# Delta rule of an RWKV-7 layer: the last level's growth interleaved with z's products, spreading behind the level's first products, and the masks for the sample chunk shared among engines

## What is computed

```python
def step(S, inp):
    r_t, w_t, k_t, v_t, kk_t, b_t = inp
    sa = jnp.einsum('bhvk,bhk->bhv', S, kk_t)
    S = S * w_t[:, :, None, :] - sa[..., None] * b_t[:, :, None, :] + v_t[..., None] * k_t[:, :, None, :]
    return S, jnp.einsum('bhvk,bhk->bhv', S, r_t)
```

## Time and profile before

| | us |
|---|---|
| timed executions | 1428.38, 1430.29, 1417.46 |
| their median | 1428.38 |
| profiled execution, its own time | 1415.87 |
| its span, first to last instruction | 1414.1 |

### The profile page before, as it was taken

One profiled execution on the slowest core, in us unless ns is written; L12 is line 12 of the kernel. 1 busy time (PEld: TensorE's weight loads), 2 busy tenths in 40 slices (PEclk: granted clock), 3 DMA queues, 4 the chain that ended last, 5 costly groups with the idle time before them and its releaser, 6 DMA issues. The chain is left out here.

```text
span 1414.1 us, 33194 instructions
## 1 busy us (share of the span) xinstructions
PE 1341.6 (95%) x13740; PEld 1178.7 (83%) x13740; DVE 768.3 (54%) x1571; ACT 634.4 (45%) x1486; POOL 240.8 (17%) x335
## 2 busy tenths in 40 slices
PE   7999999999999998999999799999999998998997
PEld 6989999888899977888887388899999997665885
DVE  6837434677771047898888444721121113776445
ACT  6725445778762124445544432521111134876224
POOL 0000000000000045777776200000001000113000
PEclk9999999999999989999999999999999998999999
DMA  6722313466679255666773381053334265330212
GB/s 215 229 66 67 105 62 115 116 176 220 194 209 268 67 110 105 134 138 145 157 156 81 116 297 54 1 203 92 92 92 111 62 167 180 101 103 24 91 41 86
DMA packets 265272, 178.44 MB, mean 126 GB/s; under 512 B 169600, under 2 KB 239168, under 8 KB 264208
## 3 DMA queue, kind: packets, MB, share of 16 engines
q1 hardware_dynamic: 233159, 161.37, 40.1%
q10 hardware_dynamic: 31968, 15.04, 3.7%
HBM read 116.21 MB, written 60.46 MB: 125 GB/s over the span
## 5 line engine op out<-in xcount | busy, mean ns | idle before, releaser
L369 PE MATMUL mix_acc<-mix_high,mix_w_high 128*128 128x364 f32 (+1 forms) x768 | 178.2, 340 | 12.3 <-ACT mix_high L435 9.9
L369 PE MATMUL mix_acc<-mix_low,mix_w_high 128*128 128x364 f32 (+1 forms) x768 | 172.0, 332 | 1.2 <-DVE mix_low L589 1.2
L369 PE MATMUL mix_acc<-mix_high,mix_w_low 128*128 128x364 f32 (+1 forms) x768 | 170.8, 331 | 0.0
L369 PEld LDWEIGHTS mix_acc<-mix_high,mix_w_high 128*128 128x128 f32 x768 | 130.1, 189 | 31.5 <-issue 28.3
L369 PEld LDWEIGHTS mix_acc<-mix_low,mix_w_high 128*128 128x128 f32 x768 | 132.9, 189 | 2.3 <-DVE mix_low L589 2.1
L369 PEld LDWEIGHTS mix_acc<-mix_high,mix_w_low 128*128 128x128 f32 x768 | 133.6, 189 | 0.2 <-DVE mix_w_low L603 0.2
L603 DVE TENSOR_TENSOR mix_w_low<-mix_wt,mix_w_high 128x1024 fp32r<-128x1024 f32 x32 | 39.2, 1224 | 126.0 <-ACT mix_w_high L441 125.7
L1605 PE MATMUL out_acc<-qkvg_room_r_high,qkvg_room_w_high 128*128 128x364 f32 (+1 forms) x320 | 105.8, 331 | 1.2 <-DVE qkvg_room_w_low L1957 1.2
L1605 PE MATMUL out_acc<-qkvg_room_r_low,qkvg_room_w_high 128*128 128x364 f32 (+1 forms) x320 | 105.1, 329 | 0.0
L1605 PE MATMUL out_acc<-qkvg_room_r_high,qkvg_room_w_low 128*128 128x364 f32 (+1 forms) x320 | 105.1, 328 | 0.0
L455 ACT ACTIVATE mix_out<-mix_acc 128x364 f32<-128x364 f32 (+1 forms) x96 | 38.3, 471 | 144.8 <-PE mix_acc L369 144.7
(11 more groups left out here) (282 smaller groups left out, 3110.6 us busy)
## 6 DMA issues: line engine op xcount, KB each, us to landing
mix_wt<-in_w_in SPq DMA_DIRECT2D x32, 512.0 KB, 4.4
qkvg_room_wt<-in_w_att SPq DMA_DIRECT2D x20, 512.0 KB, 3.6
delta_bk<-scr_bk SPq DMA_DIRECT2D x68, 128.0 KB, 3.5
delta_kr<-scr_kr SPq DMA_DIRECT2D x17, 512.0 KB, 6.7
scr_kr<-mix_outs SPq DMA_DIRECT2D x16, 512.0 KB, 3.6
scr_bk<-mix_outs SPq DMA_DIRECT2D x16, 512.0 KB, 4.4
early_xpad<-in_xpad SPq DMA_DIRECT2D x8, 548.5 KB, 8.5
scr_xg<-early_xs SPq DMA_DIRECT2D x8, 544.0 KB, 3.2
```

What stands on the lines that cost most here:

```text
L369: mm = pe.matmul(acc[:, s, k, 0:width], w[:, s, d, :], r[:, d, n0:n0 + width], start=d == 0 and q == 0, stop=d == DT - 1 and q == 2)
```

## The change

1. `make_lm` of level 0 writes each head's product to the other half of the partitions, and `keep_lm` copies it back in two halves, so `lm_kept` counts eight a chunk (`lm_copies`). `begin_z` and `end_z` write to the other half too, and `keep_z` copies z back in two halves.
2. `end_z` goes pair by pair between the pairs of the last level's `grow`.
3. `spread_blocks` of the front chunk stands behind the level-2 `make_lm`.
4. On ScalarE the root stands ahead of the first row copy; on VectorE the masks of the front chunk's first Gram products stand ahead of the last solving steps.
5. At the end GpSimd masks v for four sequences and ScalarE for four; ScalarE masks u for four and VectorE for four; VectorE makes the plain copy of u in halves, alternating with ScalarE's. z's products of the sample chunk stand ahead of the own products 0 and 1, and five warm products are gone.
6. VectorE makes one low part of weights instead of two after each of the pairs 4 to 7; the other four are made in the next stage, behind the first tokens' low part.

```diff
@@ -907,6 +907,10 @@
     return ap.rearrange("p (m o b) -> p m o b", o=2, b=8 << lev)[:, :, odd, :]
...
+def lm_copies(c, lev, g):
+    return 8 * c + (2 * g + 2 if lev == 0 else 2 * lev + g + 3)
@@ -1076,7 +1080,7 @@
                 pool.wait_ge(v_sample_loaded, 32)
-                for b in range(NB):
+                for b in range(NB // 2):
@@ -1132,7 +1136,8 @@
                         if lev < 2:
-                            mm = pe.matmul(level_bank[g][half, 32 * j:32 * j + 32], below[half, lev, pair, :],
+                            to = FLIPPED[p] if lev == 0 else half
+                            mm = pe.matmul(level_bank[g][to, 32 * j:32 * j + 32], below[half, lev, pair, :],
@@ -1142,15 +1147,17 @@
                     between(pair)
...
-        def grow(c, lev):
+        def grow(c, lev, between=lambda pair: None):
             for g in range(2):
-                pe.wait_ge(lm_kept, 6 * c + 2 * lev + g + 1)
+                pe.wait_ge(lm_kept, lm_copies(c, lev, g))
...
-                mm.then_inc(grown, 1)
+                    if j == 3:
+                        mm.then_inc(grown, 1)
+                    between(4 * g + j)
@@ -1163,25 +1170,26 @@
             for p, half in enumerate(HALVES):
-                mm = pe.matmul(chain_bank[half, 64 * pair:64 * pair + 64], grams[FLIPPED[p], c % 3, pair, p, 0, :], uv[FLIPPED[p], c % 3, pair, p, :],
+                mm = pe.matmul(chain_bank[FLIPPED[p], 64 * pair:64 * pair + 64], grams[FLIPPED[p], c % 3, pair, p, 0, :], uv[FLIPPED[p], c % 3, pair, p, :],
...
-        def end_z(c):
-            if c:
-                pe.wait_ge(s_kept, c)
-            else:
-                pe.wait_ge(zeroed, 3)
-            pe.wait_ge(z_begun, c + 1)
-            for pair in range(DT):
-                for half in HALVES:
-                    o = chain_bank[half, 64 * pair:64 * pair + 64]
-                    if c < SAMPLE:
-                        mm = pe.matmul(o, kr[half, c % 4, 0, pair, :], state[half, c % 2, pair, :], start=False, stop=True, skip_group_check=True)
-                    else:
-                        mm = pe.matmul(o, own_turned[half, pair, 0, :], unit64[half, :], start=False, stop=True, skip_group_check=True)
-            mm.then_inc(z_made, 1)
+        def end_z(c, pair):
+            if pair == 0:
+                if c:
+                    pe.wait_ge(s_kept, c)
+                else:
+                    pe.wait_ge(zeroed, 3)
+                pe.wait_ge(z_begun, c + 1)
+            for p, half in enumerate(HALVES):
+                o = chain_bank[FLIPPED[p], 64 * pair:64 * pair + 64]
+                if c < SAMPLE:
+                    mm = pe.matmul(o, kr[half, c % 4, 0, pair, :], state[half, c % 2, pair, :], start=False, stop=True, skip_group_check=True)
+                else:
+                    mm = pe.matmul(o, own_turned[half, pair, 0, :], unit64[half, :], start=False, stop=True, skip_group_check=True)
+            if pair == DT - 1:
+                mm.then_inc(z_made, 1)
@@ -1189,7 +1197,7 @@
                 pe.wait_ge(solved_wide, c + 1)
-            pe.wait_ge(z_kept, c + 1)
+            pe.wait_ge(z_kept, 2 * c + 2)
@@ -1312,26 +1320,20 @@
                 warm()
+            if 0 <= i < SAMPLE:
+                make_lm(i, 2)
             if live(front):
                 spread_blocks(front)
             if 0 <= i < SAMPLE:
-                make_lm(i, 2)
-                end_z(i)
-                grow(i, 2)
+                grow(i, 2, lambda pair: end_z(i, pair))
             if i == SAMPLE:
-                pe.wait_ge(solved_wide, SAMPLE + 1)
-                for _ in range(3):
-                    warm(solve_bank)
-                own_values((0,))
                 wait_for_values(i)
                 for pair in range(DT):
                     begin_z(i, pair)
-                own_values((1,))
-                end_z(i)
+                for pair in range(DT):
+                    end_z(i, pair)
+                own_values((0, 1))
             if behind == SAMPLE:
-                warm(solve_bank)
-                warm(solve_bank)
@@ -1358,18 +1360,17 @@
                 act.wait_ge(u_made, c)
-            act.activation(z[:], chain_bank[:, :].rearrange("p (j n) -> p j n", j=DT), ACT.Copy).then_inc(z_kept, 1)
+            src = chain_bank[:, :].rearrange("p (j n) -> p j n", j=DT)
+            for p, half in enumerate(HALVES):
+                act.activation(z[half], src[FLIPPED[p]], ACT.Copy).then_inc(z_kept, 1)
...
+                if c == SAMPLE and p == 1:
+                    act.wait_ge(u_plain_kept, 1)
                 act.activation(uv[half, c % 3, :, p, :], src[FLIPPED[p]], ACT.Copy).then_inc(u_kept, 1)
-            if c == SAMPLE:
-                act.wait_ge(below_made, 2 * SAMPLE)
-                act.wait_ge(small_made, SAMPLE + 1)
-                for p, half in enumerate(HALVES):
-                    act.activation(lower[half], src[FLIPPED[p]], ACT.Copy).then_inc(u_plain_kept, 1)
@@ -1384,8 +1385,13 @@
                     act.wait_ge(grown, 6 * (c - 1) + 2 * lev + 1 + g)
-                act.activation(blocks(lm[:, lev, 4 * g:4 * g + 4, :].rearrange("p j n -> p (j n)"), lev, 0),
-                               level_bank[g][:, 0:128].rearrange("p (m b) -> p m b", b=8 << lev), ACT.Copy).then_inc(lm_kept, 1)
+                kept = blocks(lm[:, lev, 4 * g:4 * g + 4, :].rearrange("p j n -> p (j n)"), lev, 0)
+                made = level_bank[g][:, 0:128].rearrange("p (m b) -> p m b", b=8 << lev)
+                if lev == 0:
+                    for p, half in enumerate(HALVES):
+                        act.activation(kept[half], made[FLIPPED[p]], ACT.Copy).then_inc(lm_kept, 1)
+                else:
+                    act.activation(kept, made, ACT.Copy).then_inc(lm_kept, 1)
@@ -1423,14 +1429,18 @@
                 keep_lower(front)
+            if i == SAMPLE:
+                act.wait_ge(v_sample_loaded, 32)
+                for b in range(NB // 2, NB):
+                    act.activation(v_own[:, b], v_sample[:], ACT.Copy, scale=seq_mask[:, b:b + 1]).then_inc(v_owned, 1)
...
+            if live(behind):
+                root(behind)
             if live(front):
                 keep_rows(front, 0)
-            if live(behind):
-                root(behind)
@@ -1545,6 +1555,18 @@
             dve.tensor_tensor(gated[:, c % 2], state_bank[:, :].rearrange("p (j n) -> p j n", j=DT), gate[:, c % 2], ALU.mult).then_inc(y_gated, 1)
...
+        def keep_plain_u():
+            dve.wait_ge(u_made, SAMPLE + 1)
+            dve.wait_ge(below_made, 2 * SAMPLE)
+            dve.wait_ge(small_made, SAMPLE + 1)
+            src = chain_bank[:, :].rearrange("p (j n) -> p j n", j=DT)
+            dve.tensor_copy(lower[HALVES[1]], src[HALVES[0]]).then_inc(u_plain_kept, 1)
+            dve.wait_ge(u_kept, 2 * SAMPLE + 1)
+            dve.tensor_copy(lower[HALVES[0]], src[HALVES[1]]).then_inc(u_plain_kept, 1)
+            dve.wait_ge(u_plain_kept, 2)
+            for b in range(NB // 2, NB):
+                dve.tensor_scalar(u_own[:, b], lower[:], seq_mask[:, b:b + 1], None, ALU.mult).then_inc(u_owned, 1)
@@ -1554,13 +1576,14 @@
             front, behind = i + 1, i - 1
-            if live(i):
-                solve_columns(i, range(4, 7))
...
+                solve_columns(i, range(4, 7))
                 widen_blocks(i)
+            if behind == SAMPLE:
+                keep_plain_u()
@@ -1578,8 +1601,7 @@
                         gate_y(SAMPLE)
-                    for d in range(2 * pair - DT, 2 * pair - DT + 2):
-                        ahead["rest_of_weights"](dve, d)
+                    ahead["rest_of_weights"](dve, pair - DT // 2)
@@ -1877,8 +1899,7 @@
         rest_of_tokens(0)
-        if y_tiles is None:
-            rest_of_weights(0, range(DT // 2, DT))
+        rest_of_weights(0, range(DT // 2, DT))
         rest_of_tokens(1)
         for t in range(ROW_TILES):
             if t + 2 < ROW_TILES:
```

## The result

The changed kernel takes 1488.48 us (median of four, 1483.47 to 1497.56); the kernel before took 1424.85 in the same comparison (1417.46 to 1430.29). The ratio is 1.0467 [1.0424, 1.051]: 4.7% slower, where 1416 us and "the same" were forecast.

The account below looks back on a forecast made before the run. TensorE and VectorE were taken to bound each turn together. 1415.87 + 3.9 (turns) - 1.5 (disturbed turns) - 8.2 (end) = 1410.1 us profiled, 1422.6 carried to the median; the middle, 1416 us, was named, range 1397 to 1436.

Parts of the forecast that it names:

- the turn: One chunk's round in the delta-rule stage: 15.62 us before, less 1.05, plus 1.31, giving 15.88 us.
- the merged block: z's second half interleaved with the last growth on TensorE: 1.1 us instead of 1.07 + 1.12.
- the upper bound: Interleaved z and growth at worst: 4.3 us, if each of sixteen alternations let a product run out at 0.27 us.
- The rival: Alternating 32-row and 64-row products costs TensorE up to 4.3 us a block, 1443 us in all; chance 0.07.
- the two slower rivals: Falling TensorE clock, 1444 us, chance 0.08; costly alternation of z and growth, 1443 us, chance 0.07.
- A fallen turn: Turn with TensorE's clock at 1.2 GHz after an idle gap: +1.9 us, +28 us in all; chance 0.08.
- the end: Stage's end: masks and copies shared out, updates 7.1 us sooner, 8.2 us saved in all, bounds 5 and 10.
- The new wait of VectorE: VectorE's solving starts 1.54 us behind the level-1 transpose instead of 0.23, awaiting the moved spreading: 1.31 us a turn.
- the root's wait: VectorE's 1.05 us wait before the reciprocal, for ScalarE's root, goes or nearly goes in each turn.
- The idle time ahead of `u`: TensorE idles 1.4 us a turn waiting for added growth, hiding z's second copy and a block up to 2.5 us.
- the way from there to the next stage: From the sample states' updates to the next stage: 1.1 us taken of 1.8 us of remainders removed from VectorE.
- The split `lm` copies: Level 0's `lm` copied in two halves: 1.5 us of slack before VectorE gets to the growth of level 0.

Follow-up runs that it names:

- before_rows64: The kernel before with the last growth contracting over 64 rows instead of 32, nothing interleaved; 1426.06 us, ratio 1.0003.
- rows64: The changed kernel with the last growth contracting over all 64 rows of a head instead of 32, interleaving kept; 1417.55 us, ratio 0.9953 to the kernel before.
- by_two: The changed kernel with z's products put in after every second pair of the last growth, 7 shape changes instead of 15; 1475.86 us, ratio 1.0362 to the kernel before.
- z_apart: The changed kernel with z's second half in one piece ahead of the last growth, one shape change; 1427.9 us, ratio 1.003 to the kernel before.
- end_only: The changed kernel with parts 2, 3 and 4 undone, copies in halves and changed end kept; 1420.04 us, ratio 0.9962 to the kernel before.
- diag64: The kernel before with the last growth over 64 rows and z's products between its pairs, both on the array's diagonal; 1428.17 us, ratio 1.001.
- z_halves: The kernel before with only the copy of z taken in two halves; 1422.65 us, ratio 0.9998.
- rows64_spread: The changed kernel with the last growth over 64 rows and spreading back ahead of the level-2 `lm` products; 1405.34 us, ratio 0.987; repeated, 1404.37 us, 0.9874.

## Why the prediction was wrong

**The step that failed** is the first of the turn: "By that row the merged block takes 1.1 us". The row was `u` with `y`, both of 64 rows. It took 4.0 us at the full clock, where the upper bound said 4.3, and 6.08 at the half. The remark that the contraction changes between 32 and 64 rows stood in the text and got a chance of 0.07, on the argument that blocks of the two kinds follow each other without recorded idle time at 690.80. The shapes themselves stood in the two last rows, 64*64 and 32*64, and `u` is 64*64. One change costs 0.13 us, and busy records without a gap hide that: in the kernel before, the block is 0.14 us longer for its one change (before_rows64). Price and overlap were both wrong, since the overlap needs like shape too. The Trainium skill ("TensorEngine Tiling (Array Packing)", Tiling Modes, Key Properties) says that a change of mode drains the engine. The runs agree: fifteen alternations take 1.09 us in one shape (rows64) and 4.0 in two.

**The rival was priced too low.** It allowed for 1443 us, and 1488 came, since each of the two slower rivals was priced alone. The clock fell as well, and not for the reason given, a gap of TensorE: in the turn from 700.36 TensorE was busy for 20.63 of 21.14 us. A fallen turn was put at +1.9 us, from a stretch of 6.7 us at half clock less 1.4 us of idle time; by_two's stretches last some 10 us, and it shows +3.9 (20.40 less 16.46). Fourteen turns of that are 55 us, an estimate that takes every turn as fallen, of the 75 us by which the stage's turns grew. The net loss is 63.6 because the end gained 8.

**What was right.** Without the changes of shape the turn is 15.98 us in z_apart and rows64; 15.88 was forecast. The new wait of VectorE was put at 1.31 us and is 1.23 in the undisturbed turn, 1.39 in the mean of rows64 (20.9 over 15); the root's wait is gone. That the moved spreading is a loss was right: putting it back gave 12 us, some 0.9 us a turn, less than the 1.31 of the sum because 0.46 us of the wait remained. The idle time ahead of `u` (1.4) came in rows64 and could not come in the changed kernel, where TensorE is the bound.

**The end.** Measured in end_only from the reciprocal of chunk 14 to the next stage's first copy, 771.81 to 808.82, it takes 37.0 us; before, 766.80 to 811.97, 45.2. That is 8.2 us less, as forecast, but partly by luck: the updates start 21.05 us behind that reciprocal in place of 27.00, so 6.0 sooner where 7.1 was forecast, and the way from there to the next stage is 2.2 us shorter where 1.1 was. Part of the 2.2 was no term of the sum: in the profiled kernel before, the first updates fell in a stretch at 1.2 GHz (794.50 to 797.50, granted clock 0.50), and their first eight records took 3.13 us in place of 1.93. The timeline of the end of end_only, one row or two of each engine:

```profile
790.25 2.56 ACT L1426 ACTIVATE delta_u_own<-delta_lower,delta_seq_mask 128x512 f32<-128x512 f32 x4
...
790.25 1.67 DVE L1570 TENSOR_SCALAR delta_u_own<-delta_lower,delta_seq_mask 128x512 f32<-128x512 f32 x4
...
792.86 1.93 PE L1279 MATMUL delta_level<-delta_u_own,delta_rows 64*64 64x512 f32 x8 [0.55 <-ACT delta_u_own L1426]
...
803.02 0.69 DVE L1558 TENSOR_TENSOR delta_gated<-delta_state_out,delta_gate 128x512 f32<-128x512 f32 x1
...
808.82 2.00 ACT L1809 ACTIVATE qkvg_room_r_high<-begun_work 128x1024 fp32r<-128x1024 f32 x2 [6.17 <-PEq L60]
```

They answer to the earlier trace rows: four masks each, 2.56 and 1.67 us beside each other in place of 5.00.

**The split `lm` copies** were given 1.5 us of slack. In the old order they have none and cost 0.42 us a turn. In the new order the wait for the spreading may absorb them; no run takes them out there.

## What to carry over

Before alternating two sets of matmuls, compare the tile shape that the profile prints for each: blocks of unlike shape belong one after the other, and a contraction over rows that hold zeros may buy like shape for nothing (before_rows64: 1.0003). Overlap needs like shape and different tiles; diag64 had only the first and won nothing. Put nothing between a product and the engine that waits for it, even if the product's own engine gains, and price two risks of one edit together where they can come together.

## What was not expected of the hardware

TensorE's granted clock fell to 1.2 GHz once in every turn of a stage in which the engine was 97% busy. It goes with the changes of shape inside the block: over chunks 0 to 14 of the profiled executions the clock was 0.98 in the kernel before and 0.92 in z_apart, each with one, 0.90 with three, 0.80 with seven and 0.76 with fifteen, and 0.96 to 1.00 in three kernels with fifteen alternations of one shape. One execution scatters: before_rows64 and z_halves, which time as the kernel before does, have 0.96 and 0.95. But the timed executions agree; the medians of their clocks over the whole kernel are 0.977, 0.971, 0.959, 0.937 and 0.935 in the same order, and 0.977 to 0.985 for the three. The Trainium skill ("TensorE: Matmul & The Clock Gate", What's actually happening) ties the lower clock to idle time; here it fell with no gap over 1.7 us in the stage, and none over 0.3 in the turn from 700.36. What in the changes brings it down was not found, nor why some z_apart turns fall and others don't. The timeline doesn't point at the block itself: in nine of the changed kernel's 14 turns the clock fell before the merged block began, up to 3 us (at 702.4 for the block at 702.98), and the 10 us at full clock ahead of that hold no alternation. Whether rows64_spread would gain more with level 0's copies whole wasn't tried: then they would share the diagonal with the beginning of z, and diag64's sets didn't overlap on shared tiles.
